# Sums of squares, segment sums and retention means in a kernel of three blocks: plain fp32 products against products of rounded parts

## The reference, cut to what matters

```
# first block, state-space mixer: segment sums of the log decays a = dt * A, per head and chunk of 128
#   seg[i, j] = sum of a over (j, i];  exp(seg) weighs the products of a chunk

# second kind, each of two layers
u = rms_norm(h, attn_norm)
dq, dk, dv, rq, rk, rv, rg, gq, gk, gv, gates = split(u @ w_in)
dq, dk = partial_rope(rms_norm(dq)), partial_rope(rms_norm(dk))      # heads of 64
gq, gk = axial_rope(rms_norm(gq)), axial_rope(rms_norm(gk))          # heads of 64
a = rms_norm(differential_attention(dq, dk, dv, lam), diff_subln)    # heads of 128
r = bidirectional_retention(rope(rq), rope(rk), rv)                  # linear in rv
mu  = mean(r, head);  var = mean((r - mu)**2, head)                  # head_group_norm
r = silu(rg) * (r - mu) * rsqrt(var + eps) * gain
c = grouped_query_attention(gq, gk, gv)
h = h + (sum of sigmoid(gates) * [a, r, c] @ w_branch) @ w_out
h = h + square(relu(rms_norm(h) @ w_mlp_in)) @ w_mlp_out
```

## Time and profile before

| | |
|---|---|
| time, median of 3 | 3031.07 us (3030.98 to 3031.24) |
| the profiled execution's own time | 3027.84 us |
| its span, first to last instruction | 3026.1 us |
| TensorE busy | 2959.1 us, 98% |
| VectorE busy | 1539.5 us, 51% |
| ScalarE busy | 1281.9 us, 42% |
| GpSimd busy | 432.4 us, 14% |
| mean granted clock of TensorE | 0.996 |

### The profile page before, as it was taken

How to read it: one execution, slowest core, us unless ns; L and a number is a source line. 1 busy time by engine, 2 the same in 40 slices (tenths; PEclk the granted TensorE clock), 3 DMA queues, 4 the chain that set the end, 5 groups by cost and what they waited for, 6 DMA issues and landing times. The chain is left out here.

```text
span 3026.1 us, 36184 instructions
## 1 busy us (share of the span) xinstructions
PE 2959.1 (98%) x13344; PEld 2316.1 (77%) x13344; DVE 1539.5 (51%) x2047; ACT 1281.9 (42%) x1889; POOL 432.4 (14%) x248
## 2 busy tenths in 40 slices
PE   7998999999999999999999999999999999999999
PEld 6776778888778786677777888887667777888887
DVE  3427667445754666655534551445655734453241
ACT  3556325334533455645534432234654544332231
POOL 5000000000100002211211122121221111222221
PEclk9999999999999999999999999999999999999999
DMA  7322113333323332122322333333222322333332
GB/s 188 89 71 66 55 48 98 94 96 97 104 85 102 89 98 65 48 77 80 95 70 84 98 97 95 95 97 97 60 59 71 103 72 77 97 92 97 97 97 91
DMA packets 466356, 264.20 MB, mean 87 GB/s; under 512 B 21274, under 2 KB 455292, under 8 KB 466208
## 3 DMA queue, kind: packets, MB, share of 16 engines
q1 hardware_dynamic: 460256, 251.14, 28.9%
q0 software_dynamic: 5952, 11.13, 1.4%
HBM read 254.85 MB, written 5.64 MB: 86 GB/s over the span
## 5 line engine op out<-in xcount | busy, mean ns | idle before, releaser
L767 POOL TENSOR_TENSOR wL<-wR,wH 128x1024 fp32r<-128x1024 f32 (+1 forms) x159 | 385.8, 2428 | 2462.7 <-ACT wH L731 2462.7
L731 ACT ACTIVATE wH<-wR 128x1024 fp32r<-128x1024 f32 (+2 forms) x475 | 491.2, 1034 | 423.4 <-DMA wR<-in_w_mlp_out_dram 196.5
L736 DVE TENSOR_TENSOR wL<-wR,wH 128x1024 fp32r<-128x1024 f32 (+2 forms) x316 | 377.9, 1196 | 472.9 <-ACT wH L731 447.7
L798 PE MATMUL ps<-uH,wH 128*128 128x512 f32 x1200 | 489.4, 408 | 11.2 <-POOL wL L767 6.5
L798 PE MATMUL ps<-uL,wH 128*128 128x512 f32 x1200 | 485.1, 404 | 0.0
L798 PE MATMUL ps<-uH,wL 128*128 128x512 f32 x1200 | 482.3, 402 | 0.0
L786 PE MATMUL ps<-uH,wH 128*128 128x512 f32 x976 | 384.9, 394 | 8.1 <-DVE wL L736 6.5
L786 PE MATMUL ps<-uH,wL 128*128 128x512 f32 x976 | 380.1, 389 | 0.0
L786 PE MATMUL ps<-uL,wH 128*128 128x512 f32 x976 | 380.1, 389 | 0.0
L798 PEld LDWEIGHTS ps<-uH,wH 128*128 128x128 f32 x1200 | 227.1, 189 | 79.9 <-issue 21.8
L798 PEld LDWEIGHTS ps<-uL,wH 128*128 128x128 f32 x1200 | 227.7, 190 | 62.1 <-issue 18.5
(11 more groups left out here) (471 smaller groups left out, 4157.1 us busy)
## 6 DMA issues: line engine op xcount, KB each, us to landing
wR<-in_w_in_dram SPq DMA_DIRECT2D x188, 512.0 KB, 3.7
wR<-in_w_mlp_in_dram SPq DMA_DIRECT2D x64, 512.0 KB, 4.0
wR<-in_w_mlp_out_dram SPq DMA_DIRECT2D x64, 512.0 KB, 4.0
wR<-in_ffn_w_up_dram SPq DMA_DIRECT2D x44, 512.0 KB, 3.8
wR<-in_w_branch_dram SPq DMA_DIRECT2D x24, 512.0 KB, 3.4
wR<-in_w_out_dram SPq DMA_DIRECT2D x16, 512.0 KB, 4.0
wR<-in_ffn_w_down_dram SPq DMA_DIRECT2D x16, 384.0 KB, 3.4
wR<-in_ffn_w_down_dram SPq DMA_DIRECT2D x16, 320.0 KB, 3.0
```

The lines of the kernel that those rows point to most:

```text
L731: st.f(st.e.activation(wH[:, slot, 0:n], wR[:, slot, 0:n], ACT.Copy), hi_ready, c + 1)
L736: st.f(st.e.tensor_tensor(wL[:, slot, 0:n], wR[:, slot, 0:n], wH[:, slot, 0:n].bitcast(F32), ALU.subtract), lo_ready, c + 1 if done is Non ...
L767: e.tensor_tensor(wL[:, slot, 0:n], wR[:, slot, 0:n], wH[:, slot, 0:n].bitcast(F32), ALU.subtract).then_inc(sem("lo_pool"), 1)
L798: ins = pe.matmul(o[:, :], w[:, k, :], x[:, k, :], start=s == 0, stop=s == 3 * KD - 1)
```

## The change

**The products.** "ss", "on", "rn" and "seg" become two fp32r products each, one of the rounded squares (or decays) and one of what is left, with constants stored as fp32r (`onesR`, `blkR`, `gtR`; ones and zeros are the same in both types).

**The parts.** The rounded squares come from a second Square on ScalarE with an fp32r output (`sqH`, `rmH`, `rqH`), and the rest from a subtraction on VectorE (`square_low`); TensorE waits for it (`sql_ready`, `aosq_low`, `rsq_low`). For "seg" VectorE spreads the rounded decays `avH`, and GpSimd spreads the rest `avL` into `tl` (`ssd_pool`); TensorE waits for `tl_ready` between the two products.

**Retention.** Its output is linear in v, so v is centred once for each head and token (`v_dve`, kind "rv", four tiles of a reduction and a correction on VectorE); the "rm" products and the subtraction of the mean go away, and the variance of a head now follows its own values two thirds of a chunk later.

**Order.** In the grouped stage `finish` of the tile before comes ahead of the low part of the weights, and a memset moves one tile ahead.

```diff
-def ret_steps(score, value, mean, var, fill):
+def ret_steps(score, value, var, fill):
     for h in range(4):
         for j in range(4):
             score(h, j)
             fill(2)
-        if h > 0:
-            mean(h - 1)
         fill(1)
         value(h)
-        fill(1)
-        if h > 0:
-            var(h - 1)
-        fill(1)
-    mean(3)
-    fill(5)
-    var(3)
-    fill(3)
+        fill(2)
+        var(h)
+        fill(2)
...
+        e.wait_ge(misc_ready, M("vt", 2, 3).nth)
+        st.s(e.tensor_copy(gtR[:, :], C("gt")))
+        st.w()
+        st.s(e.tensor_copy(avH[:, :, :], avec[:, :, :]))
+        st.w()
+        st.s(e.tensor_tensor(avL[:, :, :], avec[:, :, :], avH[:, :, :].bitcast(F32), ALU.subtract))
         st.w()
         e.sem_inc(sem("a_ready"), 1)
...
             o = g.open(pe)
-            g.close(pe.matmul(o[:, :], C("gt"), ta[:, n % 2, :], start=True, stop=True))
+            pe.matmul(o[:, :], gtR[:, :], ta[:, n % 2, :], start=True, stop=False)
+            pe.wait_ge(sem("tl_ready"), n + 1)
+            g.close(pe.matmul(o[:, :], gtR[:, :], tl[:, n % 2, :], start=False, stop=True))
...
+    def ssd_pool(e):
+        e.wait_ge(sem("a_ready"), 1)
+        for n in range(16):
+            c, q = n // 4, n % 4
+            if n >= 2:
+                e.wait_ge(misc_ready, M("seg", n - 2).nth)
+            e.tensor_tensor(tl[:, n % 2, :].rearrange("p (h t) -> p h t", h=4), C("le").unsqueeze(1).broadcast_to([P, 4, P]),
+                            avL[:, c, 4 * q:4 * q + 4].bitcast(F32).unsqueeze(2).broadcast_to([P, 4, P]),
+                            ALU.mult).then_inc(sem("tl_ready"), 1)
...
     def v_dve(st, kind, l):
+        e = st.e
         for j in range(VPARTS[kind][0]):
             low(st, (kind, j), l)
+            if kind == "rv" and j == VPARTS[kind][0] - 1:
+                for t in range(NT):
+                    v = vv[kind][:, t, :].rearrange("p (h d) -> p h d", h=4)
+                    e.wait_ge(sem("vv_ready"), v_count("dv", l) + t + 1)
+                    st.w()
+                    st.s(e.tensor_reduce(vsum[:, t, :], v, AX, ALU.add))
+                    st.w()
+                    st.s(e.scalar_tensor_tensor(out=v, in0=vsum[:, t, :].unsqueeze(2).broadcast_to([P, 4, P]), scalar=-1.0 / P,
+                                                in1=v, op0=ALU.mult, op1=ALU.add))
+                st.w()
+                e.sem_inc(sem("rv_ready"), 1)
             yield
+    def sums_of_parts_pe(pe, g, ones, hi, lo):
+        o = g.open(pe)
+        pe.matmul(o[:, :], ones[:, :], hi, start=True, stop=False)
+        g.close(pe.matmul(o[:, :], ones[:, :], lo, start=False, stop=True))
+    def square_low(st, low, x, hi):
+        st.w()
+        st.s(st.e.tensor_tensor(low, x, hi.bitcast(F32), ALU.subtract))
+        st.w()
...
         pe.wait_ge(sem("raw_tile"), rope_base(kind, l)[0] + x + 1)
         g = M("ss", kind, t, l=l)
-        o = g.open(pe)
-        g.close(pe.matmul(o[:, :], C("blk64"), sq[:, x % 2, :], start=True, stop=True))
+        pe.wait_ge(sem("sql_ready"), (len(TILES["g"]) + KD) * l + (len(TILES["g"]) if kind == "d" else 0) + x + 1)
+        sums_of_parts_pe(pe, g, blkR, sqH[:, x % 2, :], sqL[:, x % 2, :])
...
                 st.s(e.activation(raw[kind][:, x % 2, :], o[:, :], ACT.Copy, scale=lp[:, c:c + 1]))
+                st.s(e.activation(sqH[:, x % 2, :], o[:, :], ACT.Square))
                 g.done(st, e.activation(sq[:, x % 2, :], o[:, :], ACT.Square))
...
             st.s(e.tensor_tensor(qk[kind][:, t, :], raw[kind][:, x % 2, :], table[:, 0:S], ALU.mult))
-            if kind != "g" or x > 1:
+            if norm:
+                square_low(st, sqL[:, x % 2, :], sq[:, x % 2, :], sqH[:, x % 2, :])
+                e.sem_inc(sem("sql_ready"), 1)
+            if kind != "g":
                 low(st, (kind, t), l)
-            if kind == "g" and x == 4:
-                st.s(e.memset(partner["d"][:, :, :], 0.0))
             if x > 0:
                 finish(x - 1)
+            if kind == "g" and x > 1:
+                low(st, (kind, t), l)
+            if kind == "g" and x == 3:
+                st.s(e.memset(partner["d"][:, :, :], 0.0))
...
         def mean(h):
-            pe.wait_ge(sem("aosq_ready"), 4 * l + h + 1)
-            g = M("on", h, l=l)
-            o = g.open(pe)
-            g.close(pe.matmul(o[:, :], C("ones"), ao[:, 1, :], start=True, stop=True))
+            pe.wait_ge(sem("aosq_low"), 4 * l + h + 1)
+            sums_of_parts_pe(pe, M("on", h, l=l), onesR, rmH[:, :], aoL[:, :])
...
-        def mean(h):
-            pe.wait_ge(sem("ro_ready"), 4 * l + h + 1)
-            g = M("rm", h, l=l)
-            o = g.open(pe)
-            g.close(pe.matmul(o[:, :], C("ones"), ro[:, h % 2, :], start=True, stop=True))
         def var(h):
-            pe.wait_ge(sem("rsq_done"), 4 * l + h + 1)
-            g = M("rn", h, l=l)
-            o = g.open(pe)
-            g.close(pe.matmul(o[:, :], C("ones"), rsq[:, :], start=True, stop=True))
+            pe.wait_ge(sem("rsq_low"), 4 * l + h + 1)
+            sums_of_parts_pe(pe, M("rn", h, l=l), onesR, rqH[:, :], rmL[:, :])
```

More of the change, by code:

```diff
@@ L453, in step_marks @@
     diff_steps(mark("s"), mark("t"), mark("pv"), mark("on"), fill.take)
-    ret_steps(mark("rs"), mark("ro"), mark("rm"), mark("rn"), fill.take)
+    ret_steps(mark("rs"), mark("ro"), mark("rn"), fill.take)
     return marks
@@ L3130, in diff_act @@
                 st.w()
-                st.s(e.activation(ao[:, 0, :], o[:, :], ACT.Copy))
-                g.done(st, e.activation(ao[:, 1, :], o[:, :], ACT.Square))
+                st.s(e.activation(ao[:, 1, :], o[:, :], ACT.Square))
+                st.s(e.activation(rmH[:, :], o[:, :], ACT.Square))
+                g.done(st, e.activation(ao[:, 0, :], o[:, :], ACT.Copy))
                 st.w()
@@ L3189, in diff_dve @@
                     final_scale_dve(st, u)
+            if u >= 7 and u % 4 == 3:
+                h = u // 4 - 1
+                if h < 4:
+                    e.wait_ge(sem("aosq_ready"), 4 * l + h + 1)
+                    square_low(st, aoL[:, :], ao[:, 1, :], rmH[:, :])
+                    e.sem_inc(sem("aosq_low"), 1)
             if u >= 8 and u % 4 == 0:
@@ L3283, in ret_act @@
         decays(0)
-        for h in range(5):
+        for h in range(4):
             if h < 3:
                 decays(h + 1)
[L3287 to L3308, removed]
-                e.wait_ge(sem("rfin_ready"), 4 * l + h)
-                st.f(e.activation(brH[:, h - 1, :], ro[:, (h - 1) % 2, :], ACT.Copy), sem("bH_ready"), 27 + 20 * l + 8 + h)
+            follow("ro", h)
+            g = M("ro", h, l=l)
+            o = g.take(e)
+            if h >= 2:
+                e.wait_ge(sem("b_ready"), 27 + 20 * l + 8 + h - 1)
+            st.w()
+            st.s(e.activation(rsq[:, :], o[:, :], ACT.Square))
+            st.f(e.activation(rqH[:, :], o[:, :], ACT.Square), sem("rsq_done"), 4 * l + h + 1)
+            g.done(st, e.activation(ro[:, h % 2, :], o[:, :], ACT.Copy))
+            follow("rn", h)
+            g = M("rn", h, l=l)
+            o = g.take(e)
+            pin_act(e)
+            root_act(st, rsq[:, :], o[:, :], C("eps")[:, 1:2], 1.0 / P, g)
+            e.sem_inc(sem("rrt_ready"), 1)
+            e.wait_ge(sem("rfin_ready"), 4 * l + h + 1)
+            st.f(e.activation(brH[:, h, :], ro[:, h % 2, :], ACT.Copy), sem("bH_ready"), 27 + 20 * l + 8 + h + 1)
     def ret_dve(st, l, follow):
@@ L3327, in ret_dve @@
         exponents(0)
-        for h in range(5):
+        for h in range(4):
             if h < 3:
                 exponents(h + 1)
-            if h < 4:
-                e.wait_ge(sem("dcy_ready"), 4 * l + h + 1)
-                if h:
-                    e.wait_ge(misc_ready, M("ro", h - 1, l=l).nth)
-                for j in range(4):
-                    if j % 2 == 0:
-                        follow("rs", h, j)
-                    g = M("rs", h, j, l=l)
-                    o = g.take(e)
-                    st.w()
-                    g.done(st, e.scalar_tensor_tensor(out=rsc[:, j, :], in0=o[:, :], scalar=float(P) ** -0.5,
-                                                      in1=dcy[:, h % 2, 3 * P - P * j:3 * P - P * j + S],
-                                                      op0=ALU.mult, op1=ALU.mult))
-                    st.w()
-                    e.sem_inc(sem("rsc_ready"), 1)
-            if h > 0:
-                x = ro[:, (h - 1) % 2, :]
-                follow("rm", h - 1)
-                g = M("rm", h - 1, l=l)
+            e.wait_ge(sem("dcy_ready"), 4 * l + h + 1)
+            if h:
+                e.wait_ge(misc_ready, M("ro", h - 1, l=l).nth)
+            for j in range(4):
+                if j % 2 == 0:
+                    follow("rs", h, j)
+                g = M("rs", h, j, l=l)
@@ new lines, in ret_dve @@
+            follow("ro", h)
+            e.wait_ge(sem("rsq_done"), 4 * l + h + 1)
```

(9 more changed lines are left out.)

53 lines of the change are left out of this document (29 added, 24 removed).

## The result

The changed kernel takes 3043.32 us (median of 6 runs, 3038.44 to 3047.22) against 3030.66 us (6 runs, 3029.26 to 3031.24): a ratio of 1.0043, 95% interval 1.0032 to 1.0053. It is 0.43% slower, outside the range of the forecast, which had 13.7 us less. The profiled execution took 3044.5 us.

What follows compares the result with a forecast made beforehand. TensorE, busy 98% of the span, was taken as the bound. Savings of 31.3 us less 7.8 (layer starts), 6.8 (grouped attention) and 3.0 (first block) gave 13.7 us: 3017 us from 3031.07, range 3004 to 3027.

Steps and rivals of the forecast that it cites:

- the grouped attention: Eight differential tiles a layer: four of six TensorE waits grow about 0.65 us each, two tiles' saving written off; 6.8 us off.
- first block ("seg"): 16 "seg" products save 0.406 us each; small VectorE steps and GpSimd's tiles holding VectorE take 3 us off.
- on, rn, rm: Differential and retention phases: 16 products save 0.406 us each, eight means removed save 6.9 us, added work costs nothing.
- grouped tiles: Six tiles at each layer start: their 12 products give -2.9 us in place of the +4.9 us counted as saving.
- differential tiles: 16 tiles made during the grouped attention: 0.406 us saved a product, 6.8 us off for both layers.
- The price of products: On TensorE, a plain product of 0.86 us becomes two rounded ones of 0.227 us, saving 0.406 us.
- The subtraction is ready long before its product: Grouped attention: rope multiplication ends at 1242.99, its product starts at 1248.78; even 1.5 us later is free.
- The upper bound of 1.36 us a tile: Grouped attention: at worst the added work counts in full for all 16 tiles, 22 us.
- rival (b): Attention chain becomes the bound: 1.36 us for over half of 16 tiles, 12 us against 5.2; about 3024 us, chance 0.13.
- rival (c): GpSimd's tiles block the first block's chain through VectorE: up to 24.4 us, 3038 us; chance 0.05 slower, 0.03 within 0.2%.
- Starts of layers: Layer 0 waits of 2.1, 0.85, 1.4, 1.6 us; TensorE 1.9 us later there, 1.0 in layer 1; 7.8 us off.
- Half-clock stretches: Added half-clock stretches of TensorE behind new pauses, a part of the 0.07 chance of a time within 0.2%.

Runs made afterwards that it cites:

- the kernel with parts on the grouped tiles: The changed kernel with the differential tiles' sums of squares back to one plain fp32 product, without second Square or subtraction; 3018.86 us.
- no parts: The changed kernel with all rotated tiles' sums of squares one plain fp32 product again, in the old order, the rest kept; 3009.58 us.
- the kernel with one product for each tile: All 28 tiles' sums of squares one fp32r product of the rounded squares, low part left out, one Square, old order; 3009.17 us.
- the whole change in the old order: The changed kernel with VectorE's low parts of the weights and the clearing of the partner tiles where they stood before; 3043.07 us.

## Why the prediction was wrong

**The step that failed** is the grouped attention: "Four of them lie behind a tile's work on ScalarE or VectorE; I let these grow by about 0.65 us each, 2.6 us a layer, and write off the saving of two tiles there (0.8 us): 6.8 us off for both layers." (The 0.8 us is that of one layer: 2 x (2.6 + 0.8) = 6.8.) The saving of all 16 tiles is 6.5 us, and 1.0 arrives by the medians; the price is 28.5 us. Net +27.5 us where -6.5 + 6.8 = +0.3 was written. The other terms, each by its own kernel:

| step | forecast, us | measured, us |
|---|---|---|
| first block ("seg") | -6.5 + 3.0 = -3.5 | -3.5 |
| on, rn, rm | -6.5 - 6.9 = -13.4 | -17.0 (-14.1 in the traces) |
| grouped tiles | -4.9 + 7.8 = +2.9 | +9.3 |
| differential tiles | -6.5 + 6.8 = +0.3 | +27.5 |
| whole change | -13.7 | +12.7 |

The four measured terms add up to +16.3; together they cost 3.6 us less than one by one, which is inside the noise of four differences.

Point by point. *The price of products* was right: nothing but the expected 14 us is gained behind the attention. *"The subtraction is ready long before its product"* was right, 1.9 us for the wait. What was wrong is the cover for the work itself. The 98% on the page and 3.9 us of waits a layer (5.7 us with the two behind the six counted) made the grouped attention look bound by TensorE, with small gaps. It was already paced by the chain of maxima, exp, scale and transpose: shorter products there gain little or nothing (3009.17 against 3009.58 us), and what VectorE does in a tile stands ahead of the next maxima, so that its time counts in full. The upper bound of 1.36 us a tile was named and put aside as "the worst", and rival (b), that chain, had the right mechanism with too small a price, 3024 us. It is reached, and passed, because a longer row of steps on VectorE also meets GpSimd's low parts more often: 12.0 us of the growth. I had that lock in the earlier trace rows, inside this very stretch, and charged it to the first block alone (rival (c)), where it cost no more than the 3 us allowed.

*Starts of layers.* The four waits came as worked out, but the term was too small by 6.4 us. In the traces the starts of the kernel with parts on the grouped tiles end 5.1 us later than before, where 2.9 us was forecast, and 6.8 us later than with no parts; 2.3 us more stand in the first block, whose code is the same. Part is the stretch at half clock that follows such a wait: between 1150 and 1200 the clock falls twice with parts on the grouped tiles (granted clock 0.93), once before (0.97) and not at all with no parts (1.00), and each time can cost up to 1.7 us. And the -4.9 us of saving was taken as real; by the kernel with one product for each tile, nothing is saved there.

*Half-clock stretches* were a clause in the prediction. The trace has TensorE at the lower level for 26 us of the span before and 63 us after. At half speed that is up to 18 us, 11 of them in the grouped attentions. Not all of it reaches the end: the profiled execution of the whole change in the old order has 43 us at the lower level, 10 us less of loss, and at 3040.9 us is only 3.6 us shorter than the changed kernel's. Nor does a fall follow from the waits alone. That kernel has the waits of 1.68 and 0.67 us at the same place of layer 0, and its eight score products behind them take 1.13 us.

## What to carry to other kernels

A stretch in which the busiest engine is at 95% can still be bound by a chain through others: test it by what a shorter instruction would gain, not only by the idle time. There, price added work on the chain at its full length, and look up which of the engine's steps run beside another engine's locks: here the bill was the length plus 2.0 us for every further meeting. Then ask of a conversion where each converted product stands. Behind the attention the change gave 14 us or more, 6.9 us of it by leaving the means out; in the grouped attention the same conversion lost 27 us.

## What the runs showed of the hardware

A VectorE step with two SBUF inputs takes 0.69 us alone and 2.7 us beside GpSimd's subtraction of 1024 columns (2.55 us), but 0.69 us beside GpSimd's fill of the same tile (0.96 us). Filling instead of subtracting in the layers is worth 21.8 us by itself (3008.55 to 2986.78 us), with low parts left out. Not all of that is the sharing between VectorE and GpSimd: 12.9 us falls in the two grouped attentions, where VectorE had been held for 20.4 us. At the starts of the layers TensorE's two waits of 3.27 us for GpSimd's low part go down to 1.62 and 1.63 us, since the fill is done sooner.
